# Carrying x and the weight ring across the seven stages of a two-block network, with the norm folded into the transposing products

## What is computed

```python
for l in range(2):                                   # first kind
    h = rms_norm(x, norm_g[l])
    z = h @ w_in[l]                                  # 1024 -> 13 splits: conv, retention, attention, gates
    x = x + merged(conv(z), retention(z), attention(z)) @ w_out[l]
c_act = silu(c)
for l in range(2):                                   # second kind
    sh1, sc1, g1, sh2, sc2, g2 = split(c_act @ w_ada[l] + b_ada[l])
    h  = rms_norm(x, norm1_g[l]) * (1 + sc1) + sh1
    x  = x + g1 * (mixer(h) @ w_out[l])              # 8-head window attention, short conv, gating
    h2 = rms_norm(x, norm2_g[l]) * (1 + sc2) + sh2
    x  = x + g2 * peer_ffn(h2)                       # 128x128 experts, top 16 per head
def rms_norm(x, g): return x * rsqrt(mean(x * x) + 1e-6) * g
```

## Time and profile before

| | value |
|---|---|
| median of 3 runs | 3339.02 us (3334.98 to 3341.64) |
| the profiled execution | 3339.85 us, of which the span is 3338.1 us |
| PE (matrix products) busy | 2966.6 us, 89% of the span |
| DVE busy | 2346.7 us, 70% |
| ACT busy | 1475.2 us, 44% |
| POOL busy | 439.6 us, 13% |
| DMA | 558.91 MB, 167 GB/s over the span |

### The profile page before, as it was taken

How to read it: one execution, slowest core, us unless ns; L and a number is a source line. 1 busy time by engine, 2 the same in 40 slices (tenths; PEclk the granted TensorE clock), 3 DMA queues, 4 the chain that set the end, 5 groups by cost and what they waited for, 6 DMA issues and landing times. The chain is left out here.

```text
span 3338.1 us, 46522 instructions
## 1 busy us (share of the span) xinstructions
PE 2966.6 (89%) x17972; PEld 2633.7 (79%) x17972; DVE 2346.7 (70%) x4119; ACT 1475.2 (44%) x2250; POOL 439.6 (13%) x249
## 2 busy tenths in 40 slices
PE   6889988698999868699889999996779978999998
PEld 5778777577777657699889988885679978998887
DVE  4868987386899645398686667675559597555655
ACT  3344334234433323254664445453334565445554
POOL 0100000010000000289200000000048900000000
PEclk9999999799999878799999999997789999999999
DMA  5435544443455442255217667764145513555654
GB/s 195 162 127 189 196 177 178 161 164 139 167 199 193 155 158 101 88 173 186 95 55 246 237 231 242 261 234 164 51 141 178 186 54 101 185 181 191 206 190 158
DMA packets 128286, 558.91 MB, mean 167 GB/s; under 512 B 15115, under 2 KB 18988, under 8 KB 102572
## 3 DMA queue, kind: packets, MB, share of 16 engines
q1 hardware_dynamic: 127052, 551.14, 48.0%
q10 hardware_dynamic: 1008, 4.72, 0.4%
HBM read 547.37 MB, written 9.49 MB: 167 GB/s over the span
## 5 line engine op out<-in xcount | busy, mean ns | idle before, releaser
L1844 PE MATMUL e_ps<-k_hhi,e_hi 128*128 128x256 f32 x2304 | 651.4, 283 | 29.0 <-POOL e_lo L1829 29.0
L1844 PE MATMUL e_ps<-k_hlo,e_hi 128*128 128x256 f32 x2304 | 647.1, 281 | 0.0
L1844 PE MATMUL e_ps<-k_hhi,e_lo 128*128 128x256 f32 x2304 | 646.0, 280 | 0.0
L2102 DVE TENSOR_TENSOR e_lo<-e_raw,e_hi 128x1024 fp32r<-128x1024 f32 x394 | 482.7, 1225 | 182.7 <-ACT e_hi L1926 179.2
L1926 ACT ACTIVATE e_hi<-e_raw 128x1024 fp32r<-128x1024 f32 x544 | 570.5, 1049 | 25.1 <-DMA e_raw<-down 23.8
L727 DVE TENSOR_TENSOR f_wlo<-f_raw,f_whi 128x2048 fp32r<-128x2048 f32 x156 | 355.6, 2286 | 152.9 <-ACT f_whi L560 152.9
L1844 PEld LDWEIGHTS e_ps<-k_hhi,e_hi 128*128 128x128 f32 x2304 | 436.8, 190 | 29.9 <-POOL e_lo L1829 29.7
L1844 PEld LDWEIGHTS e_ps<-k_hlo,e_hi 128*128 128x128 f32 x2304 | 435.8, 189 | 0.0
L1844 PEld LDWEIGHTS e_ps<-k_hhi,e_lo 128*128 128x128 f32 x2304 | 435.0, 189 | 0.0
L560 ACT ACTIVATE f_whi<-f_raw 128x2048 fp32r<-128x2048 f32 x156 | 296.6, 1912 | 258.2 <-PE f_psA L430 139.9
L1829 POOL TENSOR_TENSOR e_lo<-e_raw,e_hi 128x1024 fp32r<-128x1024 f32 x150 | 384.5, 2579 | 89.4 <-ACT e_hi L1926 88.8
(11 more groups left out here) (333 smaller groups left out, 5219.0 us busy)
## 6 DMA issues: line engine op xcount, KB each, us to landing
f_raw<-ws SPq DMA_DIRECT2D x156, 1024.0 KB, 4.8
e_raw<-down SPq DMA_DIRECT2D x288, 512.0 KB, 3.5
e_raw<-up SPq DMA_DIRECT2D x256, 512.0 KB, 3.6
f_x<-ada SPq DMA_DIRECT2D x48, 512.0 KB, 3.5
s_raw<-ws SPq DMA_DIRECT2D x24, 1024.0 KB, 4.8
e_ada<-ada SPq DMA_DIRECT2D x48, 512.0 KB, 4.6
f_x<-out SPq DMA_DIRECT2D x4, 1024.0 KB, 6.1
f_const<-consts SPq DMA_DIRECT2D x2, 1104.0 KB, 7.1
```

Of the source, the lines that this page charges most:

```text
L1844: last = nc.tensor.matmul(psD(n), w, h, start=kt == 0 and i == 0, stop=kt == KT - 1 and i == 2)
L2102: V.tensor_tensor(lo[:, i % RING, :], raw[:, i % RING, :], hi[:, i % RING, :].bitcast(F32), ALU.subtract).then_inc(S["lo_dve"], 1)
```

## The change

- x gets a place of its own in SBUF for the whole program (`k_x`); so do the identity, the constants and parameters of the first layers, the modulation (`k_mod0`, `k_mod1`), the reciprocal root and the partial sums of squares. The first mixer, and each following stage, reads x where the last adds left it. x is still stored to DRAM by first layer 0 and both mixers, without a wait at the block's end, since the `ada` tiles and the peer's tiles still take its room; it is read back ahead of the last adds.
- One ring of four raw slots and three hi slots serves both first layers and both mixers; weights are one array `ws` and units have one running number. In the last units of a first layer SP loads the next stage's first four units, ACT and DVE split the first two. Peer 0 loads mixer 1's first four units among its up units and splits two. The mixers load the peer's first three units (512 KB each) into a ring that lies apart, and split them ahead of the last add.
- The norm: after each 128x512 piece of the last adds ACT squares that piece (four, scale 1/32, into four sums). POOL adds eps in the old stage (`norm_early`) and forms the root in the new one (`norm_late`). DVE makes a diagonal matrix (identity times the root, 128x128, two), and PE multiplies x by it, 16 calls of 128x128 in full fp32, in place of the multiplication on DVE and the transposes. The first unit waits for h tile by tile rather than for all of it. The peer's norm moves from the mixer's end to the peer's start.
- In mixers and peer ACT writes h in fp32 (`hv`), DVE copies it to `k_hhi` and subtracts for `k_hlo`; the next-used gain is computed behind it.
- The first layers are written out twice rather than looped over; DMA addresses are constants.
- `prepare` loads x into SBUF as its first DMA, then four weight units, constants and bias; the bias rows are made by one product on 8 partitions, copied as 8x384 and stored with a broadcast read; neither of its stores is waited for at its end.
- The last peer stage interleaves its four products with its four adds and stores x in four pieces of 256 KB.

The diff, cut:

```diff
 def first_layer(nc, env, l, inp):
             @block.sync
-                sp.dma_start(Xr[:, :, :], x_dram).then_inc(S["in_x"], 16)
-                sp.dma_start(CO[:, :], inp["consts"][:, 0:n1]).then_inc(S["in_par"], 16)
-                sp.dma_start(PA[:, :], inp["par1"][bass.ds(l, 1), :, :]...).then_inc(S["in_par"], 16)
-                sp.dma_start(BG[:, :], bias_of(2)).then_inc(S["in_bg"], 16)
-                for k in range(NRAW):
-                    load(k, k)
-                for u in range(NRAW, U1):
+                for u in range(NRAW, U1 + NRAW):
                     if u == ADA_FROM - 4:
+                        sp.wait_ge(G["c_out"], 16)
                     a = ada_tile(u + 1)
                     if a is not None:
                         if a < 2:
-                            sp.wait_ge(S["x_norm"], NT)
+                            sp.wait_ge(S["small_ready"], small["norm"] + 4)
+                            if l:
+                                sp.wait_ge(G["x_out"], 16)
-                    sp.wait_ge(S["unit_done"], u + 1 - NRAW)
-                    load(u, u % NRAW)
-                sp.wait_ge(S["ada_done"], HALF_MOD)
-                sp.dma_start(inp["mod_cols"]..., MOD).then_inc(S["out_mod"], 16)
-                sp.dma_start(Xr[:, :, :], x_dram).then_inc(S["in_x"], 16)
-                sp.wait_ge(S["out_mod"], 16)
-                sp.wait_ge(S["x_done"], 4)
-                sp.dma_start(x_dram, Xr[:, :, :]).then_inc(S["out_x"], 16)
-                sp.wait_ge(S["out_x"], 16)
+                    if u == U1:
+                        sp.wait_ge(S["ada_done"], HALF_MOD)
+                        sp.dma_start(Xr[:, :, :], x_dram if l else inp["x"]).then_inc(G["in_x"], 16)
+                        if l == 0:
+                            sp.wait_ge(S["conv_u"], 1)
+                            sp.dma_start(PA[:, :], inp["par1"][1, :, :]).then_inc(G["in_pa"], 16)
+                            sp.wait_ge(S["acc_read"], by[("g0", 1)]["n"] + 2)
+                            sp.dma_start(BG[:, :], inp["bgate"][3 + 2, :, :]).then_inc(G["in_bias"], 16)
+                        else:
+                            sp.wait_ge(S["r_og"], 8)
+                            sp.dma_start(env["par2"], inp["par2"][0, :, :]).then_inc(G["in_pa"], 16)
+                    sp.wait_ge(G["unit_done"], g0 + u + 1 - NRAW)
+                    env["load"](sp, g0 + u)
+                if l == 0:
+                    sp.wait_ge(S["x_done"], 4)
+                    sp.dma_start(x_dram, Xr[:, :, :]).then_inc(G["x_out"], 16)
             @block.tensor
-                pe.wait_ge(S["x_norm"], 2)
-                transposes(small["norm"], tmpx)
-                pe.wait_ge(S["small_read"], small["norm"] + 4)
+                pe.wait_ge(S["diag_ready"], NT)
+                for b in range(4):
+                    bank = small_bank(small["norm"] + b)
+                    for kk in range(2):
+                        for t in range(NT):
+                            c = 2 * b + kk
+                            last = nc.tensor.matmul(bank[:, kk * T + t * P:kk * T + (t + 1) * P],
+                                                    Xr[:, t, c * P:(c + 1) * P], rt[:, t, :], start=True, stop=True)
+                    last.then_inc(S["small_ready"], 1)
+                                if u == 0 and f == 0 and kt % 2 == 0:
+                                    pe.wait_ge(S["small_read"], small["norm"] + kt // 2 + 1)
             @block.scalar                      # heads; DVE's rests alike
-                    while converted[0] <= min(upto, U1 - 1):
+                    while converted[0] <= g0 + min(upto, U1 + 1):
+                    elif name == "final":
+                        for t in range(NT):
+                            act.wait_ge(S["x_done"], 2 * j + t + 1)
+                            nc.scalar.activation(tg[...], Xr[:, t, j * CH:(j + 1) * CH], ACT.Square, scale=1.0 / 32,
+                                                 accum_out=xss[:, 2 * j + t:2 * j + t + 1]).then_inc(G["x_sq"], 1)
             @block.vector
-                    V.tensor_scalar(tmpx[:, t, :], Xr[:, t, :], RS[:, t:t + 1], None, ALU.mult).then_inc(S["x_norm"], 1)
+                    V.tensor_scalar(rt[:, t, :], ident[:, :], RS[:, t:t + 1], None, ALU.mult).then_inc(S["diag_ready"], 1)

+def norm_early(nc, pool, env):
+    pool.wait_ge(G["x_sq"], 4 * k + NT)
+    nc.gpsimd.tensor_scalar(xss[:, 0:NT], xss[:, 0:NT], 1.0, EPS, ALU.mult, ALU.add).then_inc(G["x_eps"], 1)
+def norm_late(nc, pool, env):
+    pool.wait_ge(G["x_sq"], 4 * k)
+    nc.gpsimd.tensor_tensor(env["rstd"], xss[:, 0:NT], xss[:, NT:2 * NT], ALU.add).then_inc(G["x_sum"], 1)
+    nc.gpsimd.tensor_tensor(env["rstd"], env["rstd"], env["mhalf"], ALU.pow).then_inc(G["x_rstd"], 1)

 def second_mixer(nc, env, l, inp):
             @block.sync
-                with sp.Fori(1, U2 // NRAW) as i:
-                    for k in range(NRAW):
-                        sp.wait_ge(S["lo_ready"], i * NRAW + (k + 1 - NRAW))
-                        load(i * NRAW + k, k)
+                for u in range(NRAW, U2):
+                    sp.wait_ge(G["unit_done"], g0 + u + 1 - NRAW)
+                    env["load"](sp, g0 + u)
+                sp.wait_ge(S["small_read"], small["tm"] + 3)
+                for i in range(RING):
+                    sp.dma_start(q_raw[:, i, :], inp["down"][l * ND + i, :, :]).then_inc(Q["raw" + str(i)], 16)
                 sp.wait_ge(S["x_done"], 4)
-                sp.dma_start(x_dram, Xr[:, :, :]).then_inc(S["out_x"], 16)
-                sp.wait_ge(S["out_x"], 16)
+                sp.dma_start(x_dram, Xr[:, :, :]).then_inc(G["x_out"], 16)

+NEXT_LOADS = [ND + 84 + 9 * k for k in range(4)]
 def peer(nc, env, l, inp):
             @block.sync
+                    if i == ADA_UNIT + 4:
+                        sp.dma_start(Xr[:, :, :], x_dram).then_inc(G["in_x"], 16)
+                    if more and i in NEXT_LOADS:
+                        k = NEXT_LOADS.index(i)
+                        if k == 0:
+                            sp.wait_ge(S["g_lo_ready"], FREE)
+                            sp.dma_start(env["par2"], inp["par2"][l + 1, :, :]).then_inc(G["in_pa"], 16)
+                        env["load"](sp, DEPTH * U1 + U2 + k)
+                if not more:
+                    for n in range(4):
+                        sp.wait_ge(S["x_done"], n + 1)
+                        sp.dma_start(x_dram[:, t, ...], Xr[:, t, ...]).then_inc(S["out_x"], 16)

 def kernel(...):
-    with nc.Fori(0, DEPTH) as l:
-        first_layer(nc, env, l, inp)
+        for l in range(DEPTH):
+            first_layer(nc, env, l, inp)
```

739 lines of the change are left out of this document (410 added, 329 removed).

## The result

The changed kernel takes **3240.62 us** (median of four runs, 3237.26 to 3248.93) against 3338.9 for the kernel before; the ratio is 0.971, with a 95% interval of 0.9688 to 0.9733. It is 98 us faster. The forecast was 131 us faster, and the time lies 10 us above the top of the stated range.

A forecast was written before the change was run, and what follows sets the result against it. The prediction took the six seams between stages, 237.9 us together, to bound what the change could reach. Savings of 22.8 + 23.4 + 16.0 + 22.8 + 15.7 + 29.1 + 1.0 = 130.8 from 3339.85 gave 3209 us, range 3197 to 3231.

The forecast's parts named there:

- B: Seam between first layer 0 and first layer 1, 38.89 us before; forecast 16.1 us, 22.8 saved.
- C: Seam from first layer 1 into mixer 0, 39.46 us before; forecast 16.1 us, 23.4 saved.
- D and F: Seams from each mixer into its peer, 31.27 and 31.04 us before; forecast 15.3 each, 16.0 and 15.7 saved.
- E: Seam from peer 0 into mixer 1, 42.99 us before; forecast 20.2 us, 22.8 saved.
- A: Program start to the end of the first unit, 54.27 us before; forecast 25.2 us, 29.1 saved.
- Added elsewhere: Inside the stages between seams: SP's extra waits and moved loads make nothing late; no change in time.
- Norm products: In the seams, 32 fp32 instructions replace 16 transposes: 5.6 us, about 20 at the low clock; bounds 3.6 and 6.8.
- Rival 1: In the seams, norm products don't raise PE's clock: 3.4 us in six places, 3229 us; chance 0.11.
- rival 2: In four seams, pauses become so short that PE's clock never falls: −2.05 us each, 3201 us; chance 0.05.
- Rival 3: At the seams, a next stage isn't ready, its loads held or splits late: 3217 to 3235 us; chance 0.08.
- Rival 4: In the written-out first layers, straight-line code isn't supplied in time: up to 191 us lost, 3400 us; chance 0.02.
- Rival 5: In the seams, x must still be awaited somewhere: 4 us a seam return, 3233 us; chance 0.02.

The follow-up runs named there:

- e1: Changed kernel with the c_row store issued ahead of the broadcast store of the bias rows in `prepare`; 3235.67 us.
- e8: Changed kernel with the bias table stored small, then copied 128-fold by SP, and all norms scaled by DVE and transposed on PE; 3222.14 us.
- e7: Kernel before with first layers and mixers' loads written out and the first layers' weight ring placed as in the changed kernel; 3349.67 us.
- e10: Changed kernel with 64 bytes a partition left free behind h_lo, so all other tiles lie 64 bytes further from h; 3207.99 us.
- e3: Kernel before with its two first layers written out instead of looped over; 3332.76 us.
- e2: Changed kernel with bias rows made on 128 partitions by eight products and stored without a broadcast; 3244.2 us.
- e5: Changed kernel with bias rows stored as 12 KB, then copied by SP to the 128-fold table, copies outermost; 3234.74 us.
- e6: Changed kernel with the norms of first layers and mixers scaled by DVE and transposed on PE again, peers unchanged; 3243.19 us.

## Why the prediction was wrong, point by point

**What bounds the kernel** was right: the seams carried the chain, and five of six changed as computed. But "That is all that the change can reach" was wrong, see below. PE's idle time ahead of the norm products is 4.74 in B and 4.65 in C (4.8 put), 6.03 in D and F (6.2), 8.40 in E (9). The cover that was called tight in E held: DVE had 0.22 us of idle time between its last split and its first row of the adds.

**A was mis-sized**, by 16.6 of 29.1. The step that failed reads "the copy's issue falls to about 12.3, and the store's landing is waited for by no one". The issue was at 10.41; but I priced the store as its issue and put at nothing what it does to the store behind it. That next store's issue was held 14.7 us, and the block's end with it. The broadcast form stands in no row of before, so its price needed a bound on both sides and had none. That 10.41 is near 12.3 is partly luck: I had PE begin the eight products of before at 11.4, but they begin at 4.81 and take 10.60, and the one product of now had to wait until 8.07 for its input. With the hold taken away the rest of the sum holds: the mark is 27.30 in e1 and 25.66 in e8, against 25.2.

**The stages were set at nothing**, and cost 11 us against the forecast in the profiled execution, 19 in its repeat. The step that failed is the paragraph "Added elsewhere", with "nothing late" and "same ring, same order". It looked for waits, and found none to add. But the ring is the same in its order only: the change also moved the weight tiles in SBUF, which I took to be free of cost. e7 and e10 show that it was not. The place of the weights modulo 128 bytes, h being at a multiple of it, is worth some 11 us in the first layers (e7, by the traces) and 35 us in all (e10). No row of before told the direction, but a bound was there to be had: two distances, 0.1135 and 0.118, stand side by side in its trace, and 8,832 products of 256 columns (6,912 in the peers, 1,920 in the first layers) times 0.0045 are 40 us. The value that came, 0.120, was neither of them.

**Norm products.** The sum put 5.6 us; they took 4.9 to 6.4, near the bound "all low" (6.8) in C. The clock rose 2.8 to 6.0 us after they began, where the sum put their 20th for all. The first unit ran at the high clock from its start in every seam, as forecast. Rival 1 (clock not raised) and rival 2 (clock never falls) both fell; rival 1 said that no row tells transposes from too short a stretch, but seam D of the same trace did (see the norm above). The rule of the Trainium skill against the edit ("TensorE: Matmul & The Clock Gate", Terms), that transpose mode is four times faster for fp32, had the right sign and the wrong size: 3.65 us of transposes against 6.4 of products at nearly the same clock is a factor of 1.8, and seams B, C and E lose 1 to 2 us each by the edit on average over the traces, not 3.5.

**Rival 3** (not ready) fell: in seams B to F the first unit follows the norm products without idle time. **Rival 4** (code supply) fell by e3: the 4.15 us of the branch went with the loop and nothing came in their place. The Trainium skill ("Runtime: NRT & Kernel Launch", Instruction fetch mechanics) has instructions fetched ahead in order, with a stall at a branch taken out of what was fetched; the trace agrees. **Rival 5** fell.

**The end**: expected −1.0. From the first row of the last adds to the end of the span it is 8.8 us (3226.60 to 3235.41) in place of 10.0 (3328.04 to 3338.07): −1.2.

What stays open: what chooses between 0.1135 and 0.118; what part of the machine the 128 bytes belong to (the runs tell the place of the tiles, not what lies behind it; other distances than 0, 32 and 64 weren't tried, nor h moved by less than 1,024 bytes); what the 512-column products of the first layers want; and the worth of splitting and of loading ahead.

## What to carry to other kernels

When a change moves tiles, compare the start-to-start time of the busiest instruction before and after, or its count per stretch: a busy share of 100% hides a 2 to 6% slower PE, and 64 bytes of padding may give it back. Try the padding on the whole kernel, as one kind of product can lose by it while another gains. A DMA that nobody waits for still holds its queue and its share of the engines; keep a many-fold copy off a queue that has something behind it, and let its outer dimension be one that spreads. Costs that a trace doesn't show belong into the range with both ends, the places of tiles among them.

## What was not expected of the hardware

- With h at a multiple of 128 bytes, products of 256 columns start every 0.1135 or 0.118 us when the weights' tiles lie 64 bytes past a multiple of 128, every 0.120 when they lie at one, and every 0.115 to 0.123 at 32 bytes past.
- Products of 512 columns in the up units start every 0.2267 us when both operands lie at the same place modulo 128 (0, 32 or 64), and every 0.2289, once 0.2333, when they lie 64 bytes apart.
- A broadcast store of 1.5 MB with an outer dimension of 8 held the next issue on its queue for 14.7 us, made a weight load land after 18.5 us (e1), and left a stretch with a DMA share of 0.46 at 50 GB/s; the same bytes with 128 outermost landed after 5.1 (e2) and 12.4 us (e5), and nothing was held.
- 16 transposes of 3.65 us raised PE's clock with nothing behind them: it rose 2.9 us after they began (seam D of the kernel before). With products right behind, it rose after 4.7 us (seam B of e6).
- A hardware loop of two turns cost 8 us in this kernel (4 to 11 by the interval), 4 of them in the seam with the branch.
